# Attention units issued in pairs on TensorE and ScalarE of a one-core decoder block

## The reference

```python
# eight "FoX" heads: forgetting bias from a cumulated gate, causal
logits = q @ k.T * scale + (cum[q] - cum[key]); softmax over keys <= query; out = p @ v
# eight "DSA" heads: only the 256 best keys of a row by an index score take part
logits = q @ k.T * scale, others -inf;          softmax;                    out = p @ v
```

## Time and profile before

| | |
|---|---|
| median of 3 runs | 1511.62 us (1506.62 to 1514.23) |
| profiled execution, its own time | 1509.27 us |
| its span | 1507.6 us |
| PE busy | 1416.2 us, 94% |
| ACT busy | 666.5 us, 44% |
| DVE busy | 839.3 us, 56% |
| attention on PE, first L to last V | 379 to 703 us |

### The profile page before, as it was taken

One profiled execution on the slowest core, in us unless ns is written; L12 is line 12 of the kernel. 1 busy time (PEld: TensorE's weight loads), 2 busy tenths in 40 slices (PEclk: granted clock), 3 DMA queues, 4 the chain that ended last, 5 costly groups with the idle time before them and its releaser, 6 DMA issues.

```text
span 1507.6 us, 19842 instructions
## 1 busy us (share of the span) xinstructions
PE 1416.2 (94%) x7231; PEld 1205.5 (80%) x7231; DVE 839.3 (56%) x1456; ACT 666.5 (44%) x1274; POOL 709.5 (47%) x455
## 2 busy tenths in 40 slices
PE   1899899999799999998999799999999998999998
PEld 1888678888699988987788688888888886888886
DVE  5634879996567779635455733444433343515414
ACT  4523456541466656656435443333333332423421
POOL 2331312242435322280003998888888873642640
PEclk8899999999899999898899899999999999999999
DMA  9121222241624665520411122222222226643631
GB/s 380 48 74 60 77 78 91 91 150 50 170 63 112 207 201 162 140 78 29 154 43 56 50 90 85 84 84 84 84 85 84 84 71 259 226 150 138 205 126 56
DMA packets 103915, 171.73 MB, mean 114 GB/s; under 512 B 7981, under 2 KB 58341, under 8 KB 102794
## 3 DMA queue, kind: packets, MB, share of 16 engines
q1 hardware_dynamic: 103818, 170.46, 35.2%
HBM read 136.81 MB, written 33.62 MB: 113 GB/s over the span
## 4 chain that ended last, share of the span: by engine, by line
PE 82%; DVE 6%; DMA 4%; issue 2%; ACT 2%; SPq 2%; POOL 1%; DVEq 0%; POOLq 0%; ACTq 0%
PE PS L1783 22%; PE PS L1784 21%; PE PS L1785 21%; PE PS L1957 7%; PE PS L1926 3%; PE PS L1944 2%; PE PS L1945 2%; DMA rawb<-in_w_down_dram 1%; PE PS L1943 1%; DMA adar<-in_ada_w_dram 1%; DVE acc L1228 1%; PE PS L1987 1%; DVE marks_c L1365 1%; DVE XLf L1672 1%; DVE LP L1524 0%
## 5 line engine op out<-in xcount | busy, mean ns | idle before, releaser
L861 POOL TENSOR_TENSOR BS<-rawb,BS 128x1024 fp32r<-128x1024 f32 x44 | 106.9, 2434 | 127.9 <-ACT BS L1144 127.9
L848 POOL TENSOR_TENSOR WS<-WSf,WS 128x512 fp32r<-128x512 f32 x110 | 162.7, 1486 | 0.7 <-ACT WS L1088 0.7
L1088 ACT CAST WS<-WSf 128x512 fp32r<-128x512 f32 x110 | 68.4, 622 | 202.0 <-POOL WSf L838 201.1
L838 POOL TENSOR_TENSOR WSf<-rawg 128x512 f32<-128x512 f32 x55 | 77.3, 1405 | 167.7 <-PE PS L1785 166.5
L1957 PE MATMUL PS<-Vn,PT 128*128 128x64 f32 x1152 | 148.6, 276 | 0.2 <-ACT PT L1010 0.2
L1957 PEld LDWEIGHTS PS<-Vn,PT 128*128 128x128 f32 x1152 | 145.1, 199 | 0.9 <-ACT PT L1010 0.3
L1783 PE MATMUL PS<-BS,AS 128*128 128x512 f32 x352 | 138.0, 392 | 6.5 <-POOL BS L861 6.2
L1783 PE MATMUL PS<-yh,WS 128*128 128x512 f32 x352 | 137.9, 392 | 2.9 <-DVE yl L1644 2.9
L1785 PE MATMUL PS<-yh,WS 128*128 128x512 f32 x352 | 137.7, 391 | 0.0
L1784 PE MATMUL PS<-BS,AS 128*128 128x512 f32 x352 | 137.5, 391 | 0.0
L1784 PE MATMUL PS<-yl,WS 128*128 128x512 f32 x352 | 137.5, 391 | 0.0
(11 more groups left out here) (306 smaller groups left out, 3516.9 us busy)
## 6 DMA issues: line engine op xcount, KB each, us to landing
rawb<-in_w_down_dram SPq DMA_DIRECT2D x44, 512.0 KB, 3.5
adar<-in_ada_w_dram SPq DMA_DIRECT2D x32, 512.0 KB, 4.4
raw<-in_w_in_dram SPq DMA_DIRECT2D x24, 512.0 KB, 3.9
rawg<-in_w_gate_dram SPq DMA_DIRECT2D x22, 512.0 KB, 4.7
rawu<-in_w_up_dram SPq DMA_DIRECT2D x22, 512.0 KB, 4.3
gu_scratch<-Cu SPq DMA_DIRECT2D x44, 256.0 KB, 2.0
rawa<-gu_scratch SPq DMA_DIRECT2D x44, 256.0 KB, 3.6
ada<-in_ada_w_dram SPq DMA_DIRECT2D x8, 1024.0 KB, 9.4
```

Source lines behind the costliest of these rows:

```text
L838: pool.tensor_tensor(WSf[m % N_SLOT][:], left(i, mat, a), left(i, mat, b), ALU.add if sign > 0 else ALU.subtract).then_inc(ws_sum, 1)
L848: pool.tensor_tensor(lo, WSf[m % N_SLOT][:] if b else left(i, mat, a), hi.bitcast(F32), ALU.subtract).then_inc(ws_ready, 1)
L861: pool.tensor_tensor(b[:, 1, :], rawb[m % 2][:], b[:, 0, :].bitcast(F32), ALU.subtract).then_inc(gb_lo, 1)
L1088: act.copy(WS[m % N_SLOT][:, 0], src).then_inc(ws_hi, 1)
```

## The change

Two units now stand together. PE's list, per pair b, is L(2b), L(2b+1), side groups, V(2b-4), T(2b-2), V(2b-3), T(2b-1). ACT's is side groups, E(2b), K(2b-2), K(2b-1), E(2b+1). No instruction is added or removed, and no buffer, semaphore or tile size changes.

```diff
+def turned_at(b):
+    groups = [("C", ANGLE_UNITS.index(s)) for s in (2 * b, 2 * b + 1) if s in ANGLE_UNITS]
+    return groups + [("M", MOD_UNITS.index(s)) for s in (2 * b, 2 * b + 1) if s in MOD_UNITS]
 ...
@@ transposes_plan
-    for s in range(UNITS + 2):
-        if s in ANGLE_UNITS: / if s in MOD_UNITS: order.append(...)
-        if s >= 2:
-            order += [("T", s - 2, b) for b in range(len(halves(P * ((s - 2) % TT + 1))))]
+    for b in range(UNITS // 2 + 1):
+        order += turned_at(b)
+        for u in (2 * b - 2, 2 * b - 1):
+            if u >= 0:
+                order += [("T", u, i) for i in range(len(halves(P * (u % TT + 1))))]
@@ ScalarE
-                if s >= 2:
-                    for b in range(len(halves(P * ((s - 2) % TT + 1)))):
-                        evac_group(("T", s - 2, b))
-                if s < UNITS:
-                    expo(s)
+                for g in turned_at(b):
+                    evac_group(g)
+                if 2 * b == 11 * TT:
+                    roots(1)
+                if 2 * b < UNITS:
+                    expo(2 * b)
+                for u in (2 * b - 2, 2 * b - 1):
+                    if u >= 0:
+                        for i in range(len(halves(P * (u % TT + 1)))):
+                            evac_group(("T", u, i))
+                if 2 * b < UNITS:
+                    expo(2 * b + 1)
@@ TensorE
-            for s in range(UNITS + 3):
-                if s < UNITS:
-                    logits(s)
-                if 2 <= s < UNITS + 2:
-                    for b in range(len(halves(P * ((s - 2) % TT + 1)))):
-                        turn(("T", s - 2, b))
-                if s >= 3:
-                    values(s - 3)
+            for b in range(UNITS // 2 + 2):
+                if 2 * b < UNITS:
+                    logits(2 * b)
+                    logits(2 * b + 1)
+                for g in turned_at(b):
+                    turn(g)
+                for u in (2 * b - 2, 2 * b - 1):
+                    if u >= 2:
+                        values(u - 2)
+                    if 0 <= u < UNITS:
+                        for i in range(len(halves(P * (u % TT + 1)))):
+                            turn(("T", u, i))
```

More of the change, by code:

```diff
@@ L1021, in roots @@
                                bias=epsc[:], scale=1.0 / GW).then_inc(yroot, 1)
[L1023 to L1029, removed]
-                    roots(1)
-                if s >= 2:
-                    for b in range(len(halves(P * ((s - 2) % TT + 1)))):
-                        evac_group(("T", s - 2, b))
-                if s < UNITS:
-                    expo(s)
+            for b in range(UNITS // 2 + 1):
+                for g in turned_at(b):
+                    evac_group(g)
+                if 2 * b == 11 * TT:
+                    roots(1)
+                if 2 * b < UNITS:
[6 more added lines that the diff above has]
+                    expo(2 * b + 1)
             roots(0)
@@ L1963, in _ @@
             pe.wait_ge(sign_cnt, len(SIGN_TILES) * BISECT)
-            for s in range(UNITS + 3):
-                hd, t = divmod(s, TT)
-                if s < UNITS:
-                    logits(s)
[L1968 to L1971, removed]
-                if 2 <= s < UNITS + 2:
-                    for b in range(len(halves(P * ((s - 2) % TT + 1)))):
-                        turn(("T", s - 2, b))
-                if s >= 3:
-                    values(s - 3)
+            for b in range(UNITS // 2 + 2):
[10 more added lines that the diff above has]
+                            turn(("T", u, i))
             pe.wait_ge(tp_ev, len(plan))
```

## The result

The changed kernel took 1534.38 us (median of 4 runs, 1529.22 to 1541.83) against 1512.92 (1506.62 to 1517.58) of the kernel before in the same comparison: ratio 1.0148, 95% interval 1.0092 to 1.0205, so 21.5 us or 1.5% slower. The forecast was 1524, 12.4 us slower, with 1505 to 1536 as its range. The sign was right, and the size too small by 9 us. The profiled execution took 1534.62 us, against 1509.27.

A forecast was written before the change was run, and what follows sets the result against it. PE was taken to bound the kernel, full except where DVE is late. Seams -3, new wait +6, late spots +10.4 and hidden delays -1 gave +12.4 us: 1521.7 profiled, 1524 as median, range 1505 to 1536.

The forecast's parts named there:

- The seams: PE, 64 pairs: the second L's weight load is hidden behind the first; -0.05 us each, -3 us, bounds 0 and -4.5.
- The new wait: PE at T5 waits for ACT's copy K4, now behind E6, which waits for DVE's B6; +6 us, bounds 2 and 10.
- The late spots: Where DVE is already late (heads 0, 7, 8, 10 and two `query_lo`), PE loses more; +10.4 us, bounds 4 and 15.
- the same form: Heads 8 and 10 lose like head 7, where modulation waits for its DMA and T5, V4, L0 remain; about 2 us each.
- rival 3: PE's granted clock falls behind the new idle time at T5; 8 to 10 us more, 1533 us, chance 0.16.
- three signs of being wrong: T5's idle absent in heads 9 and 11; B6 starting right at L6's end in modulated heads; clock's falls changing by more than two.
- the third: Sign that the forecast is wrong: the number of PE's clock falls changes by more than two.
- Rival 4: Long runs of T and V on PE halve the clock rate, 3.1 us in each of 16 heads; +50, 1574 us, chance 0.03.
- Rival 2: Faster: two early L give DVE logits sooner, idle and half clock go; -11 us, 1501 us, chance 0.12.

The follow-up runs named there:

- e1: Changed kernel with PE's pairs kept but ACT's list as in the kernel before, apart from side groups: 1525.51 us, ratio 1.0075 to the kernel before.
- e11: Changed kernel with the row blocks modulation waits for loaded at 128 of 1024 columns, only the first two whole: 1532.1 us, ratio 1.012 to the kernel before.
- the repeated run: The changed kernel, unaltered, run once more beside the other variants: 1532.23 us, ratio 1.0131 to the kernel before.
- e9: Changed kernel with 16 added 128x64 matmuls ahead of T5 in heads 6, 8 and 10: 1526.93 us, ratio 1.008 to the kernel before.
- e10: Changed kernel with 32 added transposes of the identity ahead of T5 in heads 6, 8 and 10: 1528.45 us, ratio 1.0048 to the kernel before.
- e5: Changed kernel with ACT's copies one place earlier and POOL's prepare waiting until DVE has read the last logits: 1505.68 us, ratio 0.9932 to the kernel before.
- e6: Kernel before with only POOL's prepare waiting until DVE has read the last logits: 1503.99 us, ratio 0.9913 to the kernel before.
- e3: Changed kernel with DVE's modulation step of t = 5 moved to t = 4: 1543.49 us, ratio 1.0194 to the kernel before.
- e7: Changed kernel with DVE's modulation steps after B0, B2, B4 and B6: 1529.35 us, ratio 1.0074 to the kernel before.

## Why the prediction was right in sign and short in size

**The seams**, forecast -3 us. Head 3, which nothing disturbs, takes 18.53 us before and 18.23 after from V0 to V0. 0.30 x 16 = -4.8 us, an estimate from this one head (in e1, head 9 shows 0.31: 16.35 before, 16.04 there): the step was right, its size a little low, outside the bound of -4.5. The second L of a pair has 0.23 us at its first matmul, as forecast.

**The new wait**, forecast +6. T's entries behind idle, without the four long ones, are 11 and sum to 6.4 us. Head 9 has 1.15 and head 11 has 1.39 for 1.4; FoX heads 4 and 5 have 0.26 and 1.24 for 0.5 each; in head 5 modulation waited 0.88 us for its block. e1 confirms the cause: with K ahead of E these waits are gone.

**The late spots**, forecast +10.4. In idle time they cost 7.6: +2.2 in head 6 (3.85 for 0.59 + 1.03), +3.5 in head 8, -0.3 in head 10, +1.6 in head 0, and together 0.6 at the two `query_lo`. (The prediction calls the place of 520.51 head 7, and the earlier trace rows head 5; by the count of V they are heads 6 and 4.) In heads 0, 6 and 8 the mechanism was as forecast: "at that same moment T5 starts". For head 10 the prediction was wrong in giving it "the same form": no block is late there (the rows are with e11). Head 8 has more because its modulation ran into `prepare`. DVE and POOL in the changed kernel:

```profile
573.48 3.34 DVE L1540 SCALAR_TENSOR_TENSOR mod<-adar,cact,mod 128x1024 f32<-128x1024 f32 x1 [3.06 <-DMA adar<-in_ada_w_dram]
...
573.40 2.34 POOL L770 TENSOR_TENSOR KB<-Kd,KA 128x1024 fp32r<-128x1024 f32 x1
```

and in the repeated run, where DVE began first:

```profile
571.41 1.28 DVE L1540 SCALAR_TENSOR_TENSOR mod<-adar,cact,mod 128x1024 f32<-128x1024 f32 x1 [2.77 <-DMA adar<-in_ada_w_dram]
...
571.62 3.29 POOL L770 TENSOR_TENSOR KB<-Kd,KA 128x1024 fp32r<-128x1024 f32 x1
```

PE's gap there is 6.35 in the one and 4.01 us in the other: 0.29 from the wait for the block, 2.06 from the step itself.

**What was missed in the sum.** First, head 2: the prediction said of SP's loads and POOL's `prepare` that L7 comes earlier, "so neither is later". It did not ask what an earlier `prepare` meets. It met DVE's choice steps, B7 came late, and PE's gap at L1 of the next head (449.07) is 3.05 us. With this, idle time grows by 6.4 + 7.6 + 3.05 = 17.1, less about 1 for small old waits that went: 16.0 measured, 15.4 forecast. The match is partly luck, since head 2 fills what the late spots lack.

Second, and this is the step that failed: the sum priced gaps by their own length, and gave the clock to rival 3 with a chance of 0.16 and 8 to 10 us. Half clock in the attention rose by 34 us. PE's busy time rose by 8.5 with 4.8 saved at the seams, so the clock took 13.3. This is a remainder; the records give nearly the same by another way: PE was busy for 29.7 of the 34 us at half clock before and for 58.1 of the 68 now, and half of the 28.4 between them, the time that full clock would have saved, is 14.2. Rival 3's mechanism came true beside the forecast one, its time of 1533 is within 2 us of the measured one, and it belonged in the sum: the row at 600 to 620 us had shown it. The 1.03 us of head 6 cost nothing more in the kernel before; the 3.85 us in their place brought 13.65 us at half clock. e9 shows this by taking the gap away. 16.0 + 13.3 - 4.8 = 24.5, the attention's growth; the executions profiled are 25.3 us apart, the medians 21.5. None of the three signs of being wrong appeared, but the third was badly chosen: the clock's falls in the attention went from five to seven, a change of no more than two, while their length doubled.

Rival 4, that runs of V and T lower the clock, is excluded where it can be seen: head 3 has none of it, and in e10 12.00 us that hold 32 more turns in a row have the full clock. The Trainium skill (TensorE: Matmul & The Clock Gate, Part 4: PE-mode transpose) says that a transpose does not count as PE-busy in the same way; this head's clock did not show it. Rival 2, faster, needed K ahead of E; e1 has that, and is still 0.75% slower, since heads 2, 6 and 8 lose 7.8, 8.4 and 5.3 us in it. Most of this is `prepare` and the clock, for e5 is level with e6.

## What to carry to other kernels

When a wait on the full engine goes from several short gaps to one long gap, price the gap and the slower work behind it. Before reordering an engine that others hang on, ask of each engine that is released earlier what it will now run beside, and of each copy what it now stands behind. Here the best versions came not from the new order but from holding one helper back until DVE had read the last logits, which gave 0.9 to 1.0% in either order.

## What the runs showed of the hardware

DVE and POOL slow each other. A DVE SCALAR_TENSOR_TENSOR of 128x1024 took 1.28 us alone, and 1.7 to 3.3 beside POOL's casts and subtraction; a TENSOR_SCALAR 0.69 and 2.72; POOL's subtraction 2.36 and 3.20. The Trainium skill (SBUF — State Buffer, section SBUF: two separate sides) describes the port pair that the two share as an exclusive lock. The rows agree with it: in head 2 the TENSOR_SCALAR began at 445.15, beside a subtraction of POOL from 444.12 to 447.32, and ended at 447.87, 0.55 us after it. Which of the two pays can change from run to run: in head 8 the one that began first, by 0.08 and 0.21 us, took its usual time, and the other one waited.

Behind most idle gaps of 2 us and more PE ran at 1.2 GHz, for 3.4 to 17 us, though it was busy from the end of the gap on. Three such gaps had no lower clock behind them: 2.71 us in head 5 of e3, 2.26 in head 0 of e7, and 2.19 in head 10 of e9, 4 us after the added work. Of the shorter ones, 1.56 us in e9 and 1.72 in e10 had it, while 1.57 in the kernel before (646.00 us) and 1.76 in e3 had not. A gap's length alone does not decide it, and a gap is not the only cause: every run has a fall within 6 us of the 32 one-column products of the last M group, with no gap of 1 us in the 20 us ahead of it, for 3.4 us in the changed kernel and for 17.1 in e7. So single profiles of two kernels differ by this too.
